# TensorE's order inside an attention item: both head groups' transposes together, then the third slice of scores, then the values

## The reference, cut to what matters

```python
def block_attention(q, k, v):
    B, H, Lq, Dh = q.shape
    nb = Lq // Q_BLOCK
    qb = jnp.moveaxis(q.reshape(B, ATTN_KV_HEADS, ATTN_GROUP, nb, Q_BLOCK, Dh), 3, 0)
    ...
    def one_block(qblk):
        s = jnp.einsum('bkgqd,bksd->bkgqs', qblk.astype(jnp.float32), kf) * scale
        p = jax.nn.softmax(s, axis=-1)
        return jnp.einsum('bkgqs,bksd->bkgqd', p, vf)
    ...
```

## Time and profile before

| | us |
|---|---|
| median of 3 runs | 2234.96 (2234.25 to 2238.1) |
| profiled execution | 2232.16 |
| its span, first to last instruction | 2230.3 |
| TensorE busy | 2025.6 (91%) |
| VectorE busy | 1026.4 (46%) |
| ScalarE busy | 637.7 (29%) |
| GpSimd busy | 357.9 (16%) |
| wide items of attention | about 241.8 to 533.5 |

### The profile page before, as it was taken

The page is one execution under the profiler, slowest core; times in us unless marked ns, Lnnn a source line. Parts: engine busy times, 40 slices in busy tenths (PEclk is TensorE's granted clock), DMA queues, the critical chain, the costliest instruction groups (busy, mean ns, idle before and its releaser), DMA issues.

```text
span 2230.3 us, 40051 instructions
## 1 busy us (share of the span) xinstructions
PE 2025.6 (91%) x16767; PEld 1291.8 (58%) x16767; DVE 1026.4 (46%) x1824; ACT 637.7 (29%) x1325; POOL 357.9 (16%) x415
## 2 busy tenths in 40 slices
PE   4998999999999868887799999999999699999992
PEld 3556567676455457787656666666455544444441
DVE  2256665663687556666464223222332523333334
ACT  5222666663434323342330100100111111111112
POOL 2000100000000045553103122121000012222210
PEclk9999999999999979999999999999999599999996
DMA  9523300001100044443303332232432667698646
GB/s 333 171 76 117 84 4 1 1 2 57 29 24 0 14 66 83 66 75 68 96 0 104 72 70 57 69 73 76 162 113 76 236 190 201 185 282 230 185 76 216
DMA packets 260768, 225.39 MB, mean 101 GB/s; under 512 B 106540, under 2 KB 223600, under 8 KB 259696
## 3 DMA queue, kind: packets, MB, share of 16 engines
q1 hardware_dynamic: 249296, 183.93, 28.7%
q0 software_dynamic: 11296, 38.91, 7.7%
HBM read 174.10 MB, written 48.55 MB: 100 GB/s over the span
## 4 chain that ended last, share of the span: by engine, by line
PE 56%; DVE 4%; issue 2%; DMA 1%; ACT 1%; SPq 0%; PEld 0%; POOL 0%; DVEq 0%; ACTq 0%; POOLq 0%; PEldq 0%
PE ps L1152 17%; PE ps L1254 11%; PE ps L1195 6%; PE ps L1264 5%; PE ps L1043 3%; PE ps L1140 3%; PE ps L1049 3%; PE ps L1249 1%; PE ps L1216 1%; PE ps L861 1%; PE ps L851 1%; PE ps L1130 0%; PE ps L853 0%; DVE R L2216 0%; PE ps L1206 0%
## 5 line engine op out<-in xcount | busy, mean ns | idle before, releaser
L1152 PE MATMUL ps<-R 128*128 128x320 f32 x1280 | 353.2, 435 | 3.1 <-DVEq L1956 2.3
L1152 PEld LDWEIGHTS ps<-R 128*128 128x128 f32 x1280 | 242.7, 191 | 111.5 <-DVE R L1995 8.0
L875 PE MATMUL ps<-R 128*128 128x512 f32 (+1 forms) x816 | 301.6, 529 | 3.9 <-DVE R L1623 1.8
L1254 PE MATMUL ps<-R 128*128 x560 | 249.0, 598 | 3.4 <-ACT R L1552 2.3
L875 PEld LDWEIGHTS ps<-R 128*128 128x128 f32 x816 | 157.6, 194 | 143.0 <-issue 132.7
L1254 PEld LDWEIGHTS ps<-R 128*128 128x128 f32 x560 | 107.3, 192 | 138.6 <-issue 138.6
L1689 DVE TENSOR_SCALAR_CACHE_REDUCE R<-ps 128x512 f32<-128x512 f32 (+1 forms) x208 | 128.4, 666 | 57.2 <-PE ps L971 57.1
L1195 PE MATMUL ps<-R 128*128 128x512 f32 x320 | 141.1, 600 | 3.4 <-PEq L1182 3.4
L1264 PE MATMUL ps<-R 128*128 x280 | 126.2, 593 | 1.6 <-DVE R L2199 1.6
L990 PEld LDWEIGHTS ps<-cst,R 128*128 128x128 f32 x800 | 86.4, 142 | 57.8 <-issue 47.1
L2199 DVE COPY R<-ps 128x256 f32<-128x256 f32 x35 | 14.8, 424 | 216.4 <-PE ps L1279 216.4
(11 more groups left out here) (321 smaller groups left out, 2798.3 us busy)
## 6 DMA issues: line engine op xcount, KB each, us to landing
R<-in_w_mod_dram SPq DMA_DIRECT2D x12, 2048.0 KB, 8.9
R<-in_w_in_dram SPq DMA_DIRECT2D x46, 512.0 KB, 5.4
R<-in_w_gate_e_dram SPq DMA_DIRECT2D x16, 1024.0 KB, 6.2
R<-in_w_up_e_dram SPq DMA_DIRECT2D x16, 1024.0 KB, 10.6
R<-in_w_down_e_dram SPq DMA_DIRECT2D x16, 1024.0 KB, 9.1
R<-tu_scratch SPq DMA_DIRECT2D x40, 256.0 KB, 4.4
R<-in_x_sample_dram SPq DMA_DIRECT2D x16, 512.0 KB, 5.8
token_sums<-R SPq DMA_DIRECT2D x10, 512.0 KB, 5.2
```

The source lines that it names most:

```text
L875: last = mm(ps[:, u % 4, 0:w], w_sb[n % NW][:, k, :], hT[:, k, c0:c0 + w], start=(k == 0), stop=(k == KD - 1))
L1152: last = mm(ps[:, bank, 0:HALF], lhs[:, k, :], rhs[:, k, :], start=(k == 0), stop=(k == 3))
L1254: last = mm(ps[:, 2 + t % 2, :], hsT[t % 2][:, k, :], R[:, bass.ds(at + (RB + k * 512), 512)], start=(k == 0), stop=(k == KD - 1))
```

## The change

In each round of TensorE's loop the second group's turn is moved ahead of the third slice of scores. Waits stay with the instructions that they belong to; no other engine's program is touched. For context items the third slice is empty, and the order inside them stays as it was, but for round 8, where the third slice of the first wide item stands beside the last context item.

```diff
                     scores(i, slices(i)[0:2])
                 if 1 <= i <= NQ:
                     turn(i - 1, 0)
+                    turn(i - 1, 1)
                 if i < NQ:
                     scores(i, slices(i)[2:])
-                if 1 <= i <= NQ:
-                    turn(i - 1, 1)
                 if i >= 2:
                     values(i - 2)
                     if i % 4 == 1:
```

## The result

The changed kernel took 2246.88 us in the median of 5 runs (2243.77 to 2251.96), the kernel before 2234.96 (5 runs, 2234.25 to 2238.7): 11.9 us between the medians. The ratio on record, over all these runs, is 1.0065 (95% interval 1.005 to 1.0079); it isn't the quotient of the two medians, which is 1.0053, and in time its interval is 11 to 18 us. Forecast were 2251 us and +16.

What follows compares the result with a forecast made beforehand. TensorE was taken to bound attention; fourth items 9.0, plain items 1.3 and single places 5.8 summed to 16.1 us, giving 2248.3 from the profiled run and 2251 us as median. The 8-in-10 range was 2241 to 2263.

Steps and rivals of the forecast that it cites:

- the single places: Items 13, 15, 9 and 10 and the end of attention, together forecast to lose 5.8 us.
- Gain of 0.15 us an item: Wide items: adjacent turns save one change of kind on TensorE; scores to values priced like scores to transposes.
- Plain item +0.07: Each plain wide item: 0.15 us gained, 0.22 lost waiting for VectorE's copy to free the bank; 19 items, 1.3 us.
- The second turn's first two slices: They wait for ScalarE's copies, forecast free just before their transposes at 374.76 and 375.24: no gain, no loss.
- Fourth item +1.28: Every fourth item: VectorE's copy behind a late reciprocal, TensorE waits 1.50 us; seven items, 9.0 us; lower case +0.91 each.
- Item 13, +1.4: Extra ScalarE work holds up the second turn; the third scores now follow the wait, and that work begins 0.4 later.
- Item 15, +1.3: VectorE's eleven small operations after item 14's last copy start 1.53 us later, delaying score pieces and copy by 1.1 to 1.2.
- Items 9 and 10, +2.7: First two wide items: lost cover for ScalarE (+0.9), and VectorE's output product behind a later exponential; range 0 to 4.
- The end, +0.4: After attention's last item the exponentials end 0.4 us later.
- only the changes of kind count: Rival: VectorE's copy comes in time everywhere, 31 items gain 0.15 us each, 4.7 in all: 2230 us; 4 in 100.
- gains and waits cancel: Rival: VectorE's wait is met only in fourth items, at 0.5 us; 2.3 us in all, 2237 us; 5 in 100.
- The clock falls: Rival: waits of 1.5 us lower TensorE's clock in eight fourth items, costing 13.6 us: 2265 us; 12 in 100.

Runs made afterwards that it cites:

- e1: Changed kernel, with the copy of the first turn's third slice moved from VectorE to ScalarE: 2234.84 us, against 2231.73 for the kernel before.
- e6: Changed kernel, with VectorE's copy of the first turn's third slice behind two pieces of scores instead of four: 2234.79 us, against 2232.80 before.
- e3: Kernel before, with the second turn ahead of the third slice of scores only in every fourth round: 2237.80 us, against 2231.73 before.
- e2: Changed kernel, with VectorE's reciprocal moved behind the copy of the first turn's third slice: 2241.43 us, against 2231.73 before.

## Why the prediction was right, step by step

Right were the direction, the mechanism and, within a tenth, the size: 16.1 us summed, 15.5 in the wide part. That the two are so near is in part luck, since misses of opposite sign cancel: the seven fourth items measured 8.1 us (9.0 forecast), the 19 plain ones 2.3 (1.3), the single places 5.2 (5.8). By its steps:

- *Gain of 0.15 us an item, with scores before values at the old price.* Held. The third scores take 1.06 us to the values (384.75 to 385.81), just as they took to the transposes in the earlier trace rows. No run has the gain alone: where VectorE's copy no longer binds (e1, e6), a plain item is 8.65, still 0.13 over the 8.52 that the gain alone would give.
- *Plain item +0.07.* Measured +0.11. The wait was where the prediction put it. These are VectorE's copy and the last slice's first two transposes in the changed kernel's plain item (timelines cut short, the second row from 384.22 on):

```profile
383.42 0.68 DVE L1706 COPY R<-ps 128x512 f32<-128x512 f32 x1
384.16 0.44 PE L990 MATMUL ps<-cst,R 128*128 128x128 f32 x2
```

TensorE goes on at 384.16, 2.45 us behind the turn's first transpose (381.71); forecast were 2.46 (373.39 to 375.85). What the sum lacked comes behind it: from there to the third scores it takes 0.59 us (to 384.75), where the prediction had 0.53 (375.85 to 376.38). After the wait the first two transposes are 0.17 us apart and not 0.11, as they are at each change of kind.
- *The second turn's first two slices: "nothing to be had there, nothing lost".* Wrong, though it costs nothing in the changed kernel, where VectorE's later copy sets the pace. It is 0.10 of the 0.13 us that stay in e6's plain item. ScalarE's copy of the first slice and the second turn's first transpose there (timelines cut short, the second row from 376.68 on):

```profile
375.83 0.60 ACT L1425 ACTIVATE R<-ps 128x512 f32<-128x512 f32 x1 [0.46 <-PE ps L990]
376.57 0.30 PE L990 MATMUL ps<-cst,R 128*128 128x128 f32 x1
```

The copy ends at 376.43 and TensorE begins 0.14 us later, 1.44 behind the first transpose at 375.13; without a wait it would be 12 x 0.109 + 0.06 = 1.37. The next transpose follows at 376.71, another 0.03 late. The prediction had a margin of 0.06 us there and no row for the delay from ScalarE to TensorE.
- *Fourth item +1.28.* Measured +1.15. The chain was right link by link; I had the first exponential 0.25 us behind the maximum, it came 0.19 behind (387.15 to 387.34), and it took 1.57 us to the next operation (387.34 to 388.91) where I had 1.66. So the reciprocal stood at 2.17, not at 2.35: 0.18 us less, and 0.06 more for the same restart as in the plain item. e3 shows the lower case of the prediction (+0.91) as +0.95.
- *Item 13, +1.4:* +1.31. Its hole is 3.15 us now and was 1.83: the difference of 1.32 is the cover that the third scores gave, 1.06, and ScalarE's later start, 0.26 (the second turn begins 6.60 us into the round, 289.58 − 282.98, and did at 6.34).
- *Item 15, +1.3:* +1.22. VectorE's small operations reach to 306.74 and the first score piece stands at 306.77 instead of 1.17 behind the round's start at 304.48, that is 1.12 late. e1 and e6 remove it without touching those operations.

```profile
306.55 0.19 DVE L1755 COPY bg<-R 128x40 f32<-128x40 f32 x1
306.77 0.69 DVE L1688 TENSOR_SCALAR_CACHE_REDUCE R<-ps 128x512 f32<-128x512 f32 x1
```

- *Items 9 and 10, +2.7:* 9 lost 1.18 and 10 lost 1.55; item 8, which the prediction left out, gave 0.37 back: +2.36. For item 10 the prediction had VectorE's output product alone; its rows under e1 show as long a wait for ScalarE (0.65) as for VectorE (0.64).
- *The end, +0.4:* 21.27 − 20.96 = +0.31.
- *The base.* I added the sum to the median of before, 2251; the medians differed by 12 us on the first occasion (5 runs of each) and by 16 on the second (6 and 23). So few runs can't decide between these; that the wide part is 15.5 us longer, the same to 0.04 us in two profiles, is the firmer number.

The rivals: *only the changes of kind count* is refuted by the 1.05 us wait, *gains and waits cancel* by the ratio of 1.0065. *The clock falls* didn't happen in fourth items: the granted clock was 1.00 over the whole wide part of the changed kernel, and over 300 to 548 us in particular, with six fourth items and their waits of 1.05 us in it. Outside the fourth items it was near: item 13's hole lowered it in e2 and e6.

```profile
300.00:548.00 248.00, 238.98 (x2306) 166.52 (x2304) 142.03 (x434) 145.79 (x238) 14.27 (x14) 1.00 0.01 2
```

By the Trainium skill (TensorE: Matmul & The Clock Gate, Part 4), transposes don't count as TensorE being busy in the same way; in the changed kernel 24 of them in a row, with a wait of 1.05 us among them, never lowered the clock (1.00), so this trace doesn't bear that rule out. The Trainium skill's rule that a change of tiling mode drains TensorE (TensorEngine Tiling (Array Packing), Key Properties) agrees in sign with the 0.15 us at one change fewer.

## What to carry to other kernels

Where two groups of work share a few buffers, what stands between them on the bound engine is the cover for the engine that empties the buffers. Before moving it, count in the *other* engine's queue what stands ahead of the copy that frees the buffer, for each kind of round, since a rare operation at the head of that queue (here one 0.2 us reciprocal behind a long chain) costs ten times as much as in a plain round. If the order has to change, the copy's place or its engine has to change with it: e6 and e1 took 11.8 and 13.2 us off the changed kernel's wide part with one edit each, which only brings it back to near the kernel before (296.77 and 295.42 against 293.06). And read distances between repeated starts, which repeat to 0.01 us, rather than whole times, which spread over some 10 us.

## What the hardware showed that I had not expected

A hole of the same length, 3.15 us, at the same place of the program (item 13), lowered TensorE's granted clock to 0.50 in two profiles (e2, e6) and not in three (the changed kernel, its repetition, e1). Item 13 took 14.3 us in the two and 12.7 to 12.8 in the three. So the hole, 1.3 us longer than before's 1.83, made the item 1.3 us longer and, sometimes, another 1.6 us through the lower clock. With so few profiles I can't say whether that hangs on the kernel or changes between executions of one.
